# The low part of a weight half, made one step later on VectorE in a mixture-of-experts decoder layer

## The chip, the cores and the metric

The kernel runs on 1 core of one Trainium2 chip. The metric is the device time in microseconds of the whole program, the median over runs. All of it is one launch: a decoder layer with attention, a recurrent block and a mixture of experts.

## The reference, cut to what matters

```python
def _moe(h, w_router, e_bias, w_gate, w_up, w_down, ws_gate, ws_up, ws_down):
    ...
    scores = jax.nn.sigmoid(hf.astype(f32) @ w_router.astype(f32))
    ...
    _, idx = lax.top_k(jnp.where(emask, sel, -jnp.inf), TOP_K)
    ...
    def body(acc, blk):
        toks, bw, e = blk
        xb = hp[toks]
        yb = (jax.nn.silu(xb @ w_gate[e]) * (xb @ w_up[e])) @ w_down[e]
        return acc.at[toks].add(yb.astype(f32) * bw[:, None]), None
```

There are 2048 tokens of 1024 numbers, 64 experts of width 256, and each token goes to 8 experts. The pairs of token and expert are sorted by expert and padded to blocks of 128. With the inputs drawn here the routing gives 31 experts two blocks and 33 experts three, 161 blocks in all, and no expert has one.

## The kernel before, in words

The change lies in the expert stage, the function `experts`, which takes the span from about 886 to 2377 us. Its loop goes over the blocks in turns of two: block n = 0 of a turn (k = 0) is called an even step here, n = 1 an odd step. There are 162 steps. A step gathers 128 rows of h, forms G = x [gate | up] (128 x 512), H = silu(gate part) * up part * pair weight (128 x 256), transposes H and forms Y = H w_down (128 x 1024), which GpSimd adds to the sums in DRAM by a scatter.

Every product is made with numbers split in two, a high part rounded to fp32r and a low part, the difference. So a product takes three passes on TensorE: high by high, high by low, low by high. ScalarE makes the high parts, VectorE the low parts by a subtraction. This holds for the rows x (`xT_hi`, `xT_lo`), for the transposed H (`HT_hi` by line 2489, `HT_lo` by line 2590) and for the weights of an expert, in three pieces: piece 0 is the gate half of `gu_split`, piece 1 its up half, piece 2 the down weights (`d_hi`, `d_lo`). The subtraction of a weight piece is line 2528, called by `split(entry, n)` for piece n.

The weights sit in two raw slots and two split slots. At the first block of an expert the pieces of the *next* expert are split into the other slot. `when_first(engine, words[i], body)` is a branch at run time: it runs `body` only if block i is the first of its expert. In step s, `words[n]` is the block of the step, `words[n + 1]` the one behind it. For an expert whose first block is f, VectorE makes pieces 0 and 1 of the next expert at the end of step f - 2, and piece 2 early in step f.

All engines run through lists written by hand and meet on semaphores. TensorE's step is: the low pass of G for the next block (`gate_up_low`, line 2659), Y of this block (line 2697, whose third pass in each half reads `HT_lo`), the high passes of G for the block two steps on (`gate_up_high`, line 2645, which waits for the low parts of gate and up), and the H transposes of the next block (`turn_H`, line 2666, psH), in odd steps also transposes of the gathered rows (psX, psW). VectorE's step is:

```python
s.wait(dve, HThi_s)
nc.vector.tensor_tensor(HT_lo[:], ...)
when_first(dve, words[n], lambda: split(words[n], 2))
low_x(s.turn + 2, k)
...
product(s.n + 2, 1 - k, s.turn + 1 + k)
if k == 0:
    turn_x(s.turn + 2)
when_first(dve, words[n + 2], lambda: split(words[n + 2], 0))
when_first(dve, words[n + 2], lambda: split(words[n + 2], 1))
```

`product` makes H of the next block (line 2567), `turn_x` transposes the gathered rows of the odd blocks on VectorE (lines 2512 and 2514, only in even steps), after four gathers by GpSimd (line 1669) have landed. ScalarE's step is HT_hi, xT_hi, an index, silu, the high parts of gate and up where due (line 2444), the two halves of y, the high part of down where due. SP's queue reloads a raw slot's gate and up (line 2359) when the low parts of both are made (`gulo_s`), and its down weights when theirs is made.

Of the kernel before, what the change touches and what calls it, by code (L numbers as in the profile page):

```python
# [61 lines left out]
def carry_wait(eng, passed):  # L62


    eng.sem_inc(passed, 1)
# [2133 lines left out]
def experts(nc, passed, w_gate, w_up, w_down, ident, htab, hcut, sums, table, n_turns, idx, pidx, tails_s, xg, gi, gi_s, x_in, acc_out, gu, guhi_s, gulo_s, wgu, wd, loaded, y, si, added,  # L2199
# [6 lines left out]
    with ExitStack() as ctx:  # L2206
# [58 lines left out]
        def within(v, low, high):  # L2265
            return nc.s_assert_within(v, low, high, skip_runtime_bounds_check_because="the table's fields have these ranges")
# [29 lines left out]
        def entries(eng, first, n):  # L2296

            ap = table[0:1, first:first + n] if isinstance(first, int) else table[0:1, bass.ds(first, n)]
            return [Entry(v) for v in load(eng, ap, (1 << FIRST_BIT + 1) - 1)]
# [3 lines left out]
        def parts(raw, slot):  # L2303

            def piece(t, at, columns):
                return t[:, bass.ds(at, 1) if not isinstance(at, int) else slice(at, at + 1), :, columns].rearrange("p a k n -> p (a k) n")

            for h, columns in enumerate((slice(0, FE), slice(FE, 2 * FE))):
                yield piece(runs_view(wgu)[:, :, h], raw, slice(0, FE)), piece(gu_hi, slot, columns), piece(gu_lo, slot, columns)
            yield tuple(piece(t, at, slice(0, D)) for t, at in ((wd, raw), (d_hi, slot), (d_lo, slot)))  # L2310

        def when_first(eng, entry, body):

            with eng.If(entry.first() > 0):
                body()
            with eng.Else():
                eng.sem_inc(passed, 1)
# [186 lines left out]
        def _(dve):  # L2504
# [25 lines left out]
            block0, block1 = entries(dve, 0, 2)  # L2530
# [7 lines left out]
            def split(entry, n):  # L2538

                raw = within(entry.next() & 1, 0, 1)  # L2540
                src, hi, lo = list(parts(raw, 1 - entry.slot()))[n]
                if n == 2:
                    dve.wait_ge(dhi_s, entry.rank() + 1)
                else:
                    dve.wait_ge(guhi_s, entry.rank() * GU_SPLITS + n + 1)
                carry_wait(dve, passed)
                low(n, src, hi, lo)
# [32 lines left out]
            low_x(1, 1)  # L2580
            when_first(dve, block0, lambda: split(block0, 1))
            when_first(dve, block1, lambda: split(block1, 0))
            when_first(dve, block1, lambda: split(block1, 1))

            def body(i):
                words = entries(dve, i * TURN, TURN + 2)
                for n, s, k in steps(i):

                    s.wait(dve, HThi_s)
                    nc.vector.tensor_tensor(HT_lo[:], psH[:, 0:FE].rearrange("p (a b) -> p a b", a=2), HT_hi[:],  # L2590
                                            ALU.subtract).then_inc(HTlo_s, 1)
                    when_first(dve, words[n], lambda: split(words[n], 2))
                    low_x(s.turn + 2, k)
                    s.wait(dve, H_s)
                    if k == 0:
                        pair_weight(words[n + 2], s.turn + 2, 0)
                        pair_weight(words[n + 1], s.turn + 1, 1)
                    product(s.n + 2, 1 - k, s.turn + 1 + k)
                    if k == 0:
                        turn_x(s.turn + 2)  # L2600
                    when_first(dve, words[n + 2], lambda: split(words[n + 2], 0))
                    when_first(dve, words[n + 2], lambda: split(words[n + 2], 1))

            turns(dve, body)

        @block.tensor
# [733 lines left out]
```

## Time and profile before

| | |
|---|---|
| median of 3 runs | 2500.54 us (2498.16 to 2504.78) |
| the profiled execution | 2502.44 us, span 2500.6 us |
| TensorE (PE) busy | 2345.8 us, 94% of the span |
| VectorE (DVE) busy | 1659.6 us, 66% |
| ScalarE (ACT) busy | 1263.4 us, 51% |
| GpSimd (POOL) busy | 980.9 us, 39% |
| granted TensorE clock | 0.976 of full speed |
| DMA | 551.13 MB, mean 220 GB/s |

Busy time is the time in which an engine has an instruction under way; register and branch instructions don't count. The idle time of an engine that is not the bottleneck costs nothing by itself. Matmuls are pipelined, so the lengths of two neighbours overlap, and steps are best measured from start to start.

### The profile page before, as it was taken

What the parts mean: (1) busy time and instruction counts of PE and PEld (TensorE: products, weight loads), DVE (VectorE), ACT (ScalarE), POOL (GpSimd) and SP (SyncE); (2) the same over time, 40 slices, a digit from 0 to 9 for tenths busy, and PEclk for the clock granted to TensorE, in tenths of its full rate; (3) what the DMA queues carried; (4) which work ended last, traced back from release to release, by engine and by line L of the source; (5) the groups of instructions that cost most, each with busy time, mean ns of one, the idle gap of its engine ahead of it and who ended that gap; (6) DMA issues with size and microseconds to landing.
All of it is one profiled execution on the core that took longest, in us unless ns stands there. A gap on an engine that the chain in (4) does not pass through costs nothing. (4 is left out here: it accounts for less than half of the span.)

```text
span 2500.6 us, 49354 instructions
## 1 busy us (share of the span) xinstructions
PE 2345.8 (94%) x11266; PEld 1900.4 (76%) x11268; DVE 1659.6 (66%) x2220; ACT 1263.4 (51%) x2025; POOL 980.9 (39%) x772
## 2 busy tenths in 40 slices
PE   8899999989998799999999999999999999999966
PEld 6576777668886677888778887787878888887844
DVE  6685867758877766666666666656666657656337
ACT  4525253532325655555555555555655556655334
POOL 0010101011110155555555555555645556655437
PEclk9999999989998899999999999999999999999989
DMA  7243434465656479888897878888888789987796
GB/s 253 76 168 122 136 118 144 135 223 187 226 204 210 157 240 279 242 231 255 273 269 230 262 222 259 263 266 262 268 254 236 222 252 290 272 271 213 177 248 202
DMA packets 165327, 551.13 MB, mean 220 GB/s; under 512 B 31344, under 2 KB 56080, under 8 KB 144784
## 3 DMA queue, kind: packets, MB, share of 16 engines
q1 hardware_dynamic: 109696, 355.03, 39.9%
q0 software_dynamic: 54960, 195.27, 32.6%
q8 instruction: 36, 0.59, 0.1%
q14 instruction: 27, 0.22, 0.0%
q10 hardware_dynamic: 608, 0.02, 0.0%
HBM read 394.99 MB, written 155.25 MB: 220 GB/s over the span
## 5 line engine op out<-in xcount | busy, mean ns | idle before, releaser
L2645 PE MATMUL psG<-gu_split,xT_hi 128*128 x2624 | 626.2, 391 | 3.4 <-ACT xT_hi L2421 1.9
L2645 PEld LDWEIGHTS psG<-gu_split,xT_hi 128*128 128x128 f32 x2624 | 495.0, 189 | 107.6 <-issue 4.1
L1669 POOL DMA_INDIRECT xg<-hcut,gi x332 | 418.4, 1260 | 201.5 <-ACT gi L2432 113.9
L2659 PE MATMUL psG<-gu_split,xT_lo 128*128 x1304 | 342.3, 404 | 0.9 <-issue 0.9
L2590 DVE TENSOR_TENSOR HT_lo<-psH,HT_hi 128x256 fp32r<-128x256 f32 x162 | 68.7, 424 | 379.6 <-ACT HT_hi L2489 371.3
L2528 DVE TENSOR_TENSOR gu_split<-raw_gu,gu_split (+1 forms) x127 | 284.3, 2281 | 44.7 <-issue 27.0
L2659 PEld LDWEIGHTS psG<-gu_split,xT_lo 128*128 128x128 f32 x1304 | 232.9, 188 | 44.6 <-issue 2.5
L2406 POOL DMA_INDIRECT acc<-y,si x81 | 184.4, 2277 | 160.2 <-ACT y L2498 146.3
L2444 ACT ACTIVATE gu_split<-raw_gu x126 | 234.5, 1909 | 25.0 <-issue 18.3
L2697 PE MATMUL psY<-d_hi,HT_lo 128*128 x648 | 202.9, 394 | 31.7 <-DVE HT_lo L2590 31.5
L2489 ACT ACTIVATE HT_hi<-psH 128x256 fp32r<-128x256 f32 x162 | 62.2, 384 | 286.6 <-PE psH L2666 261.4
L2697 PE MATMUL psY<-d_hi,HT_hi 128*128 x648 | 201.8, 393 | 0.7 <-issue 0.5
L2697 PE MATMUL psY<-d_lo,HT_hi 128*128 x648 | 200.1, 390 | 0.0
L2512 DVE STREAM_TRANSPOSE xF<-xg 128x1024 f32<-128x1024 f32 x82 | 176.8, 2157 | 34.6 <-DMA xg<-hcut,gi 34.6
L1662 POOL DMA_INDIRECT xg<-htab,gi x83 | 81.8, 985 | 289.2 <-DVE pairw L2558 233.4
L2528 DVE TENSOR_TENSOR d_lo<-raw_d,d_hi (+1 forms) x64 | 146.7, 2293 | 44.4 <-issue 43.5
L2697 PEld LDWEIGHTS psY<-d_hi,HT_lo 128*128 128x128 f32 x648 | 120.0, 189 | 66.0 <-issue 42.5
L2406 POOL DMA_INDIRECT second<-y,si x81 | 145.8, 1800 | 26.3 <-issue 26.3
L2697 PEld LDWEIGHTS psY<-d_hi,HT_hi 128*128 128x128 f32 x648 | 121.0, 188 | 30.0 <-issue 3.9
L950 PE MATMUL psP<-xT_hi,wring 128*128 128x512 f32 x512 | 131.6, 407 | 11.2 <-ACT xT_hi L468 3.6
L2697 PEld LDWEIGHTS psY<-d_lo,HT_hi 128*128 128x128 f32 x648 | 121.9, 188 | 26.6
L418 POOL TENSOR_TENSOR OS<-QK 128x256 f32<-128x256 f32 x15 | 11.0, 735 | 316.4 <-ACT QK L560 316.4
(404 smaller groups left out, 4102.5 us busy)
## 6 DMA issues: line engine op xcount, KB each, us to landing
raw_gu<-in_w_gate_dram SPq DMA_DIRECT2D x64, 1024.0 KB
raw_gu<-in_w_up_dram SPq DMA_DIRECT2D x64, 1024.0 KB
raw_d<-in_w_down_dram SPq DMA_DIRECT2D x64, 1024.0 KB
wring<-split_d SPq DMA_DIRECT2D x24, 1024.0 KB, 5.7
second<-blank SPq DMA_DIRECT2D x17, 512.0 KB, 6.7
split_d<-wring POOLq DMA_DIRECT2D x8, 1024.0 KB, 4.2
raw_d<-mixed SPq DMA_DIRECT2D x16, 512.0 KB, 5.6
xt<-in_x_dram SPq DMA_DIRECT2D x16, 512.0 KB, 5.7
```

Source lines behind the costliest of these rows:

```text
L950: m = nc.tensor.matmul(u.tile[:], w_[:, w, k, :], xT[x_][:, k, :], start=(n == 0), stop=(n == len(passes) - 1))
L1662: nc.gpsimd.indirect_dma_start(out=to[:], out_offset=None, in_=htab, in_offset=bass.IndirectOffsetOnAxis(ap=at[:, 0:1], axis=0)).then_inc( ...
L1669: nc.gpsimd.indirect_dma_start(out=to[:, g, 0:PIECE], out_offset=None, in_=hcut.rearrange("r a w -> (r a) w"), in_offset=bass.IndirectOffs ...
L2406: nc.gpsimd.indirect_dma_start(out=sums[k], out_offset=bass.IndirectOffsetOnAxis(ap=si[k][:, 0:1], axis=0), in_=y[k][:], in_offset=None, c ...
L2444: nc.scalar.activation(dst, src, ACT.Copy).then_inc(done, 1)
L2489: nc.scalar.activation(HT_hi[:], psH[:, 0:FE].rearrange("p (a b) -> p a b", a=2), ACT.Copy).then_inc(HThi_s, 1)
L2512: nc.vector.transpose(xF[:, 0:KC, :].rearrange("p c (g j) -> p c g j", g=QUADS), xg[1][:, :, 0:FEATS].rearrange("p g (i c) -> p c g i", c=KC))
L2528: nc.vector.tensor_tensor(dst, src, hi, ALU.subtract).then_inc(dlo_s if n == 2 else gulo_s, 1)
L2590: nc.vector.tensor_tensor(HT_lo[:], psH[:, 0:FE].rearrange("p (a b) -> p a b", a=2), HT_hi[:], ALU.subtract).then_inc(HTlo_s, 1)
L2645: nc.tensor.matmul(psG[slot][:], xT_hi[slot][:, c, :], right[:, bass.ds(w, 1), c, :].rearrange("p a n -> p (a n)"), start=(n == 0 and c == ...
L2659: m = nc.tensor.matmul(psG[slot][:], xT_lo[slot][:, c, :], gu_hi[:, bass.ds(w, 1), c, :].rearrange("p a n -> p (a n)"), start=False, stop= ...
L2697: m = nc.tensor.matmul(psY[:, h, :], left[:, c, :], right[:, bass.ds(w, 1), c, h * 512:(h + 1) * 512].rearrange("p a n -> p (a n)"), start ...
```

## The change

The subtraction for piece 1, the up half, no longer follows that for piece 0 at the end of a step. It stands in the next step, directly behind HT_lo, under the same condition (there the same block is `words[n + 1]`). The one for the second block's expert in the prologue goes away, since the first step of the loop now makes it.

```diff
             when_first(dve, block0, lambda: split(block0, 1))
             when_first(dve, block1, lambda: split(block1, 0))
-            when_first(dve, block1, lambda: split(block1, 1))
...
                     nc.vector.tensor_tensor(HT_lo[:], psH[:, 0:FE].rearrange("p (a b) -> p a b", a=2), HT_hi[:],
                                             ALU.subtract).then_inc(HTlo_s, 1)
+                    when_first(dve, words[n + 1], lambda: split(words[n + 1], 1))
                     when_first(dve, words[n], lambda: split(words[n], 2))
                     low_x(s.turn + 2, k)
...
                     when_first(dve, words[n + 2], lambda: split(words[n + 2], 0))
-                    when_first(dve, words[n + 2], lambda: split(words[n + 2], 1))
```

On VectorE, at the start of the loop's body (the even step), the change puts the branch and the subtraction of piece 1 behind HT_lo; `-` is before, `+` the change, and lines shift by one:

```order
 L1126 REGISTER_ALU
-L2590 TENSOR_TENSOR HT_lo<-psH,HT_hi 128x256
+L2589 TENSOR_TENSOR HT_lo<-psH,HT_hi 128x256
+L2314 REGISTER_ALU
+L2314 COMPARE_AND_BRANCH
+L2545 REGISTER_ALU x2
+L2545 ISA
+L2528 REGISTER_ALU x3
+L2528 ISA
+L2528 REGISTER_ALU
+L2528 ISA x2
+L2528 TENSOR_TENSOR gu_split<-raw_gu,gu_split 128x8x256
```

HT_lo itself stays first in the even step; ahead of the branch for the down weights there now stands one more.

On VectorE, where the even step ends and the odd step begins, behind the subtraction of piece 0:

```order
 L2314 UNCONDITIONAL_BRANCH
 L2316 UNCONDITIONAL_BRANCH
+L2589 TENSOR_TENSOR HT_lo<-psH,HT_hi 128x256
 L2314 COMPARE_AND_BRANCH
 L2545 REGISTER_ALU x2
```

The two rows at the end belong to the branch of piece 1, which is followed by its subtraction. A few rows on, behind that subtraction, HT_lo stood before:

```order
 L2314 UNCONDITIONAL_BRANCH
 L2316 UNCONDITIONAL_BRANCH
-L2590 TENSOR_TENSOR HT_lo<-psH,HT_hi 128x256
-L2314 REGISTER_ALU
 L2314 COMPARE_AND_BRANCH
 L2543 REGISTER_ALU x3
```

So in the odd step HT_lo moved ahead of the subtraction of piece 1, and nothing else changed places. No other engine's order changes.

## Rows read from the trace of the kernel before

**Rows 1.** waits, whole span (engine, tile and line, awaited: us in total, times, longest)

```profile
PE psY L2697 <- DVE HT_lo L2590: 31.5, 21, 2.3
```

**Rows 2.** timeline, one late step (start us, length us, engine, line, operation; idle before)

```profile
1569.65 0.38 PE L2666 MATMUL psH<-ident,H 128*128 128x128 f32 x2
...
1570.62 0.38 ACT L2489 ACTIVATE HT_hi<-psH 128x256 fp32r<-128x256 f32 x1 [1.69 <-PE psH L2666]
...
1572.15 2.29 DVE L2528 TENSOR_TENSOR d_lo<-raw_d,d_hi  x1 [0.69 <-issue]
...
1573.85 3.73 ACT L2444 ACTIVATE gu_split<-raw_gu  x2 [0.53 <-issue]
...
1576.27 2.18 DVE L2512 STREAM_TRANSPOSE xF<-xg 128x1024 f32<-128x1024 f32 x1
...
1578.56 4.45 DVE L2528 TENSOR_TENSOR gu_split<-raw_gu,gu_split  x2
1579.09 0.38 PE L2666 MATMUL psH<-ident,H 128*128 128x128 f32 x2
...
1579.51 0.38 ACT L2489 ACTIVATE HT_hi<-psH 128x256 fp32r<-128x256 f32 x1 [0.89 <-PE psH L2666]
...
1582.93 0.42 DVE L2590 TENSOR_TENSOR HT_lo<-psH,HT_hi 128x256 fp32r<-128x256 f32 x1
1583.26 1.22 DVE L2520 TENSOR_TENSOR xT_lo<-xF,xT_hi 128x1024 fp32r<-128x1024 f32 x1
1583.49 0.70 PE L2697 MATMUL psY<-d_hi,HT_lo 128*128 x2 [1.27 <-DVE HT_lo L2590]
...
1584.39 0.48 DVE L2567 SCALAR_TENSOR_TENSOR H<-psG,pairw,sg 128x256 f32<-128x256 f32 x1
...
1589.03 0.38 PE L2666 MATMUL psH<-ident,H 128*128 128x128 f32 x2
```

**Rows 3.** timeline, an odd step that waits for nothing

```profile
1521.39 0.39 PE L2666 MATMUL psH<-ident,H 128*128 128x128 f32 x2
...
1529.83 0.38 PE L2666 MATMUL psH<-ident,H 128*128 128x128 f32 x2
```

**Rows 4.** timeline, an odd step in which the low part is slightly late

```profile
931.03 0.39 PE L2666 MATMUL psH<-ident,H 128*128 128x128 f32 x2
...
933.59 0.47 DVE L2590 TENSOR_TENSOR HT_lo<-psH,HT_hi 128x256 fp32r<-128x256 f32 x1
...
939.77 0.38 PE L2666 MATMUL psH<-ident,H 128*128 128x128 f32 x2
```

**Rows 5.** timeline and windows, the longest wait and TensorE's clock behind it

```profile
2281.16 1.19 PE L2697 MATMUL psY<-d_hi,HT_lo 128*128 x2 [2.29 <-DVE HT_lo L2590]
...
2281.20:2284.70 3.50, 3.50 (x9) 2.79 (x10) 1.34 (x2) 0.69 (x2) 2.59 (x4) 0.52 0.89 197
```

**Rows 6.** timeline, two even steps, each behind an odd step without a wait

```profile
1105.89 0.38 PE L2666 MATMUL psH<-ident,H 128*128 128x128 f32 x2
...
1107.92 0.38 ACT L2489 ACTIVATE HT_hi<-psH 128x256 fp32r<-128x256 f32 x1 [2.76 <-remote]
...
1922.96 0.38 PE L2666 MATMUL psH<-ident,H 128*128 128x128 f32 x2
...
1925.68 0.38 ACT L2489 ACTIVATE HT_hi<-psH 128x256 fp32r<-128x256 f32 x1 [3.44 <-remote]
...
1933.48 0.39 PE L2666 MATMUL psH<-ident,H 128*128 128x128 f32 x2
```

**Rows 7.** windows, six experts in a row without a wait

```profile
2052.00:2159.00 107.00, 107.00 (x511) 88.96 (x510) 79.01 (x84) 70.66 (x108) 69.85 (x42) 1.00 0.96 296
```

**Rows 8.** timeline, GpSimd's scatter beside VectorE and alone

```profile
1097.99 3.15 POOL L2406 DMA_INDIRECT acc<-y,si  x1 [4.08 <-ACT y L2498]
...
1099.88 1.26 DVE L2520 TENSOR_TENSOR xT_lo<-xF,xT_hi 128x1024 fp32r<-128x1024 f32 x1
...
2110.81 1.59 POOL L2406 DMA_INDIRECT acc<-y,si  x1 [1.51 <-ACT y L2498]
```

## The prediction

> **What bounds the kernel now.** The profile's page comes first: TensorE is busy for 94% of the span, so only time in which it waits can be won. The waits of TensorE on other engines come second. In the expert stage one of them counts: the product with the low part of H (line 2697) waits for VectorE's subtraction (line 2590) 21 times, 31.5 us in all, 2.3 us at most [rows 1]. The timeline around one such wait comes third [rows 2]. A step runs from one pair of H transposes on TensorE to the next. The even step starts at 1569.65 and lasts 9.44 us. Near its end VectorE turns the next rows (1576.27) and makes two low parts in one go, 4.45 us from 1578.56. The odd step begins at 1579.09; ScalarE has the high part of H started at 1579.51, so VectorE could go on at about 1579.9, but it starts HT_lo only at 1582.93, directly behind the second low part. TensorE has the products before it done and sits idle for 1.27 us until 1583.49. The step lasts 9.94 us; an odd step without a wait lasts 8.44 [rows 3]. So a listed wait of 1.27 costs 1.50, which is 0.23 more than the list says.
>
> Why 21 times: the inputs give 31 experts of two blocks and 33 of three. VectorE is late when an even step holds three low parts, the one of the down weights (1572.15 in [rows 2]) and the two that follow, which needs an expert of two blocks that starts at an even block. Leaving out the first expert, there are 21. Where the even step has only the last two, HT_lo starts 2.56 us after the transposes at the latest, and the step takes 8.74, or 0.30 too long [rows 4]; six steps look like this. Of this I also read the limit: HT_lo may start about 2.56 - 0.30 = 2.26 us after the transposes before TensorE feels it. The longest wait has a price of its own: behind it the granted clock was 0.52 for 3.5 us [rows 5], its lower level of 1.2 GHz, which loses about 1.7 us.
>
> **The change, part by part.** The same instructions are issued in the same number; one subtraction of 2.29 us per expert moves from ahead of HT_lo to behind it.
>
> *What goes.* The two low parts take 4.45 us and one alone takes 2.29 [rows 2], so HT_lo comes 2.16 us earlier: at 1580.77, or 1.68 after the transposes, where 2.26 is allowed. All waits up to 2.16 vanish: 31.5 + 21 x 0.23 = 36.3 us. The six slightly late steps give 6 x 0.30 = 1.8, the slow clock 1.7. Together 39.8 us. About three waits lie near or above 2.16; I leave 0.3 us in each, 1.0 in all.
>
> *What the moved part delays.* In the odd step it now stands ahead of the low part of x and of H, but there it stood already, since all three are behind it in VectorE's order today as well. HT_lo alone overtakes. Their starts in [rows 2] stay, while TensorE arrives 1.5 us sooner. H is made by 1584.39 + 0.48 = 1584.9, and TensorE's transposes would come at 1589.03 - 1.50 = 1587.5: 2.6 us of cover. In steps where VectorE was idle ahead of HT_lo, the part begins 0.69 us behind it (the gap that such a branch leaves, 1572.15 in [rows 2]) and pushes x and H by some 3 us. The even step of [rows 2] already holds a low part at that very place and its H is in time, so this costs nothing.
>
> *One more untaken branch.* Each step now tests one condition more between HT_lo and the down weights' low part. No row has the price of an untaken branch alone. It lies between 0 and the 0.69 of a gap that holds a taken one; I take 0.3, since much less is executed. In the even step this pushes the chain (down part, x, H, turn, first low part) and puts HT_lo at 1.98 of 2.26. At 0.69 it would be 2.37, and 21 steps lose 0.1 each.
>
> *TensorE's own wait.* gate_up_high asks for both low parts, but for the block two steps on. With two blocks or more in every expert the moved part is ready one whole step ahead. Nothing is lost there.
>
> *SP's queue.* The gate and up reload waits for the second low part, so it starts later: by HT_lo alone in [rows 2], some 0.4 us, and by up to 4 where VectorE was idle ahead of HT_lo. The slot is read again two experts on: ScalarE's split at 1573.85 recurs after 19.4 us per expert, so 29 us pass, and 26 without the waits. The three megabytes at the 296 GB/s of [rows 7] need about 11 us. That covers the delay, and costs nothing. Nor does the faster pace run into the DMA: six experts of two blocks from odd starts ran back to back at 0.96 DMA share with TensorE busy for 107.00 of 107.00 us [rows 7].
>
> *What is late next.* ScalarE. In the even step behind a late odd step its high part of H starts 0.97 us after the transposes [rows 2]. Behind an odd step without a wait it starts 2.03 after them, and once 2.72 [rows 6], with nothing in the timeline to explain it. That delay runs down VectorE's chain to the next HT_lo. With 0.97 the next HT_lo is at 1.98, no wait. With 2.03 it is at 3.04, or 0.8 too late. The change turns all late odd steps into clean ones, so it brings this about itself. Per step the cost is between 0 and 0.8; a late step helps the next one, so I take the middle, 0.4, for 21 steps: 8.4 us. At 2.72 TensorE itself waits: that even step took 10.52 instead of 9.44, which is 1.08 [rows 6]. I expect two more of these, 2.2 us; the bounds are none and five.
>
> *Sum.* 39.8 - 1.0 - 8.4 - 2.2 = 28.2 us. The profiled execution took 2502.44 (span 2500.6), so it would take 2474.2. The median of the three runs is 1.9 lower, 2500.54, and goes to about **2472 us**.
>
> **Rivals.** (a) *The whole wait goes:* ScalarE stays at 0.97. 38.8 us are won, 2462. For it: the late starts may hang on where the row gathers stand against the loop's top, and that moves too. Against it: every clean odd step with this pattern that I read has ScalarE late.
>
> (b) *Half comes back:* ScalarE's delay at its upper bound, 21 x 0.8 + 5 x 1.08 = 22.2 us, so 16.6 are left, 2484; with the branch at 0.69 as well, 2486.
>
> (c) *The gathers come late.* GpSimd's scatter took 3.15 us and ended at 1101.14, in the moment in which VectorE's low part of x ended (1099.88 + 1.26); alone it takes 1.59 [rows 8]. So VectorE's subtractions hold GpSimd back, and behind the scatter stand the four gathers whose rows VectorE turns in the even step. Today these subtractions end 5.4 us into a step of 9.94 (at 1584.5, by 1583.26 in [rows 2] and its 1.2 us), 4.5 before the next transposes; afterwards 5.8 into 8.44, which is 2.6 before. If all of the 1.9 us reached the turn at 1576.27 and then HT_lo, less the 0.28 of room, 21 steps would lose 34 us: 2506, about no change. It decides once the gathers land later than 6.6 us into the even step. Against it: the window of [rows 7] has this contention and no wait. The Trainium skill, SBUF — State Buffer, Who interferes with whom, says that a VectorE instruction with two SBUF inputs contends only with a GpSimd instruction that reads SBUF, and infers that descriptor generation is not held up by tensor_tensor. By that inference this rival costs nothing and the sum stays 2472; the row of 3.15 us speaks against it.
>
> (d) *The other side, slower:* ScalarE's high part of H starts at 2.7 in every even step behind an odd one that now holds such a low part. There are 37. TensorE loses 37 x 1.08 = 40 us, HT_lo 21 x 0.8 = 17, against 38.8 won: 18 slower, 2519. It decides somewhere between 2.03 and 2.72 us behind the transposes. Against it: 2.03 is what [rows 6] shows for an ordinary one, and only a few are at 2.7.
>
> (e) *No real move:* HT_lo stays late because the first low part alone ends too late. The rows say 1.68 against 2.26, so this would need a chain a microsecond longer than shown: 2500.
>
> **How the numbers follow.** Forecast 0.60, (a) 0.20, (b) 0.09, (c) 0.04, (d) 0.04, (e) 0.03. A measurement of this kernel can tell about 0.3%, 7.5 us, from no change. Faster by more: the first three, 0.89. Within: (c) and (e), 0.07. Slower: (d), 0.04. The range runs from the full gain with a little over, 2460, to (b) with the branch, 2487; it leaves out (c), (d), (e) and edges.
>
> **What would show it.** In the changed profile the wait of line 2697 for HT_lo should fall from 31.5 to under 12 us. HT_lo in odd steps should begin about 1.7 to 3.0 us after the transposes, followed directly by one low part of 2.29; only one should stand ahead of it. Odd steps of the late kind should last 8.4 to 9.2 instead of 9.94. ScalarE's high part in even steps should start 1 to 2 us after the transposes, and its waits and TensorE's on it should have grown. The turn should rarely wait for gathers in even steps behind late ones. I am wrong if odd steps stay above 9.5, if the turn waits for DMA where it did not, or if many even steps last over 10 us.

## The result, and the profile after

| | before | changed |
|---|---|---|
| median, beside each other | 2500.1 us (2498.16 to 2504.78, 4 runs) | 2458.78 us (2457.51 to 2465.86, 4 runs) |
| ratio, 95% interval | | 0.9838, 0.9815 to 0.9861 |
| the profiled execution's span | 2500.6 us | 2455.7 us |
| expert stage, from the first to the last H transposes | 886.0 to 2377.6: 1491.6 us | 877.4 to 2332.6: 1455.3 us |
| TensorE busy | 2345.8 us | 2333.2 us |
| granted clock | 0.976 | 0.977 |

The change won 41.3 us where 28 were forecast, and the median lies just below the range. The two profiled executions differ by 44.9 us: 36.3 in the expert stage and 8.6 ahead of it. The 8.6 are not the change's. In the other profiled executions below, whatever the kernel, the stage began anywhere from 875.5 to 885.8 us (the changed kernel's own at 876.0 to 883.8), and the part behind it was equal (123.0 and 123.1).

Waits of TensorE in the changed kernel, the row that answers to [rows 1] (31.5 us, 21 times):

```profile
PE psY L2696 <- DVE HT_lo L2589: 3.6, 5, 1.0
```

The timeline of the same even and odd step as [rows 2], in the changed kernel:

```profile
1542.83 0.38 PE L2665 MATMUL psH<-ident,H 128*128 128x128 f32 x2
...
1543.24 0.38 ACT L2489 ACTIVATE HT_hi<-psH 128x256 fp32r<-128x256 f32 x1 [1.15 <-PE psH L2665]
1543.66 0.42 DVE L2589 TENSOR_TENSOR HT_lo<-psH,HT_hi 128x256 fp32r<-128x256 f32 x1 [2.82 <-issue]
1545.14 2.29 DVE L2528 TENSOR_TENSOR d_lo<-raw_d,d_hi  x1 [1.06 <-issue]
...
1551.56 2.29 DVE L2528 TENSOR_TENSOR gu_split<-raw_gu,gu_split  x1
1552.34 0.38 PE L2665 MATMUL psH<-ident,H 128*128 128x128 f32 x2
...
1553.73 0.44 DVE L2589 TENSOR_TENSOR HT_lo<-psH,HT_hi 128x256 fp32r<-128x256 f32 x1
1554.33 2.29 DVE L2528 TENSOR_TENSOR gu_split<-raw_gu,gu_split  x1 [0.15 <-issue]
...
1557.67 0.48 DVE L2567 SCALAR_TENSOR_TENSOR H<-psG,pairw,sg 128x256 f32<-128x256 f32 x1
...
1560.76 0.38 PE L2665 MATMUL psH<-ident,H 128*128 128x128 f32 x2
```

One low part stands ahead of HT_lo in the odd step, one behind it. HT_lo starts 1.39 us after the transposes (1553.73 - 1552.34), where [rows 2] has 3.84, and the step lasts 8.42 instead of 9.94. H is ready 2.6 us ahead of the next transposes.

What was not expected stands in the even steps. The same two as in [rows 6], where ScalarE's high part of H came 2.03 and 2.72 us after the transposes, look like this in the changed kernel:

```profile
1092.71 0.38 PE L2665 MATMUL psH<-ident,H 128*128 128x128 f32 x2
...
1093.13 0.38 ACT L2489 ACTIVATE HT_hi<-psH 128x256 fp32r<-128x256 f32 x1 [1.15 <-PE psH L2665]
...
1884.43 0.38 PE L2665 MATMUL psH<-ident,H 128*128 128x128 f32 x2
...
1884.92 0.39 ACT L2489 ACTIVATE HT_hi<-psH 128x256 fp32r<-128x256 f32 x1 [1.21 <-PE psH L2665]
...
1893.89 0.39 PE L2665 MATMUL psH<-ident,H 128*128 128x128 f32 x2
```

It comes at 0.42 and 0.49, and the second step takes 9.46 instead of 10.52. In the changed kernel the high part starts at 0.51 or earlier in 79 of 80 even steps; in the kernel before it was later than 0.7 in 37 of them.

The releaser at the end of the row names the cause. In [rows 6] it is "remote", an event without an instruction that just ended; here it is the transposes themselves. The trace's semaphore events say it outright (the times are from the start of the transposes, in the even step of 1105.89 in the kernel before and of 1092.71 in the changed one):

```
event                                   before   changed
TensorE: H transposes done              2.01     0.40
TensorE: pair weights transposed        2.73     0.51
TensorE: x transposes done, first half  2.82     1.24
TensorE: x transposes done, second half 2.90     2.73
TensorE: low pass of G done             3.24     3.24
```

ScalarE started at 2.03 in the first, right behind the signal. So it was never late itself. TensorE's completion signal for the transposes was, while its matmul records and the signal of the next product were on time in both. This is called the late signal below. (In the changed kernel the signals behind the first two can be held as well, 2.73 where 1.40 is the rule; that touches the high part of x alone.)

The chain of VectorE hangs on it. In the even step of [rows 2] the signal is 0.55 us late. HT_lo and the down part stand 0.55 later for it, and so should x, H, the turn, the low parts and the HT_lo that TensorE waits for in the odd step; how much of it arrives there is measured by the unused subtraction below.

### The profile page after: what moved, and what is told of

It is laid out like the page before. It is cut to its first block and busy times, and to the rows that moved or that the text cites. A ratio compares the mean times of both kernels' runs of the same rounds, so it can differ in the third digit from the quotient of the medians.

```text
span 2455.7 us, 49353 instructions
## 1 busy us (share of the span) xinstructions
PE 2333.2 (95%) x11267; PEld 1898.1 (77%) x11268; DVE 1670.5 (68%) x2220; ACT 1268.9 (52%) x2025; POOL 980.6 (40%) x772
## 5 line engine op out<-in xcount | busy, mean ns | idle before, releaser
L1669 POOL DMA_INDIRECT xg<-hcut,gi x332 | 447.1, 1347 | 212.5 <-ACT gi L2432 122.0
L2528 DVE TENSOR_TENSOR gu_split<-raw_gu,gu_split (+1 forms) x127 | 289.8, 2282 | 78.1 <-issue 67.9
L2406 POOL DMA_INDIRECT acc<-y,si x81 | 146.9, 1813 | 136.8 <-ACT y L2498 115.9
L2512 DVE STREAM_TRANSPOSE xF<-xg 128x1024 f32<-128x1024 f32 x82 | 177.7, 2166 | 21.0 <-DMA xg<-hcut,gi 20.6
L2528 DVE TENSOR_TENSOR d_lo<-raw_d,d_hi (+1 forms) x64 | 146.7, 2293 | 63.7 <-issue 62.9
L2406 POOL DMA_INDIRECT second<-y,si x81 | 156.1, 1927 | 25.8 <-issue 24.2
```

Source lines behind the costliest of these rows:

```text
L1669: nc.gpsimd.indirect_dma_start(out=to[:, g, 0:PIECE], out_offset=None, in_=hcut.rearrange("r a w -> (r a) w"), in_offset=bass.IndirectOffs ...
L2406: nc.gpsimd.indirect_dma_start(out=sums[k], out_offset=bass.IndirectOffsetOnAxis(ap=si[k][:, 0:1], axis=0), in_=y[k][:], in_offset=None, c ...
L2512: nc.vector.transpose(xF[:, 0:KC, :].rearrange("p c (g j) -> p c g j", g=QUADS), xg[1][:, :, 0:FEATS].rearrange("p g (i c) -> p c g i", c=KC))
L2528: nc.vector.tensor_tensor(dst, src, hi, ALU.subtract).then_inc(dlo_s if n == 2 else gulo_s, 1)
```

## The experiments

Times are medians; the kernel before was timed beside each set of runs.

### Which half of the deferral does it, and is it the reload

Four kernels of one set, the kernel before at 2499.54 (2493.86 to 2509.29). The first is the changed kernel again.

> The change as it is, on this chip beside the others. 2457 to 2466 us. If the stages ahead of the expert stage run level with before here, then 8.6 us of the 44.9 us between the two first profiles are chance of these two executions; if they are again some 9 us shorter, the change acts there too.

2462.86, ratio 0.985 (0.982 to 0.987). The stage took 1457.5.

The second defers piece 1 only into odd steps:

```diff
+                    if k == 1:
+                        when_first(dve, words[n + 1], lambda: split(words[n + 1], 1))
...
-                    when_first(dve, words[n + 2], lambda: split(words[n + 2], 1))
+                    if k == 1:
+                        when_first(dve, words[n + 2], lambda: split(words[n + 2], 1))
```

> Only the up low part that used to stand at the end of an even step is moved behind HT_lo of the odd step; the one at the end of an odd step stays where it was. Theory A (the gain is HT_lo overtaking a low part in the 21 crowded odd steps): nearly all of the gain of the change, 30 to 45 us against before. Theory B (a good part of the gain comes from the even step, where the moved low part lets something else go earlier): less than 25 us.

2460.35, ratio 0.984 (0.982 to 0.987): the whole gain. It doesn't tell the overtaking of HT_lo from the late signal, since the signal is on time here too in all but five even steps.

The third defers it only into even steps (the same with `k == 0`).

> The mirror: only the up low part at the end of an odd step is moved into the next even step. Theory A: no change, within 4 us of before, and 21 waits for HT_lo of 1.2 to 2.3 us stay. Theory B: 10 us or more are won.

2513.03, ratio 1.005 (1.003 to 1.007): 13 us slower, where at most 4 were expected. The late odd step of [rows 2] in it:

```profile
1582.82 0.38 PE L2668 MATMUL psH<-ident,H 128*128 128x128 f32 x2
...
1586.98 0.40 DVE L2589 TENSOR_TENSOR HT_lo<-psH,HT_hi 128x256 fp32r<-128x256 f32 x1
...
1587.53 0.70 PE L2699 MATMUL psY<-d_hi,HT_lo 128*128 x2 [1.58 <-DVE HT_lo L2589]
...
1593.10 0.38 PE L2668 MATMUL psH<-ident,H 128*128 128x128 f32 x2
```

HT_lo starts at 4.16 where [rows 2] has 3.84, and the step takes 10.28 instead of 9.94. The only thing added to VectorE's crowded even steps is one untaken branch. Ahead of the down part the idle time is 1.06 us in the even step of the changed kernel above, against 0.69 in [rows 2]: an untaken branch costs 0.37 us there. Here it lies on the path of every late step. Three stretches ran at a granted clock of 0.50 behind their waits (3.4, 6.8 and 3.4 us), against one in the kernel before, and the longest step took 14.31. That isn't all of the loss: of the 16.4 us that the stage grew, 9.1 lie in odd steps and 7.3 in even ones, of which seven lasted 9.9 to 11.5 us, against four of 10.0 to 10.6 in the kernel before.

The fourth is the kernel before with a later reload. SP waits in addition until ScalarE has taken up the next expert's down split:

```diff
+                            sp.wait_ge(free_s, before)
...
+                act.sem_inc(free_s, 1)
```

> VectorE's order is that of before. SP's reload of gate and up waits also for ScalarE to reach the down split of the next expert, so it starts about 2.8 us ahead of the even step's transposes instead of 5.6. Theory R (ScalarE's late high part of H at the loop's top comes from the reload's traffic, and the change cured it by issuing the reload later): the high part of H starts 0.4 to 0.6 us after the transposes in all even steps; the four even steps of 10.0 to 10.6 us are gone and the crowded odd steps shorten by about 0.5 us each, 10 to 16 us won in all. Rival (the lateness follows VectorE's or GpSimd's order): ScalarE stays at 1.0 to 2.9 us, time within 4 us of before.

2515.6, ratio 1.007 (1.005 to 1.010). The gate reload now started 2.9 us ahead of the even transposes in most steps and the up reload 1.4, instead of 5.6 and 5.1, and HT_hi was still at about 0.95 behind waits. Behind short odd steps it was mostly at 2.9 to 3.0, where the kernel before has 1.4 to 2.9. So a later reload doesn't cure the signal, but it isn't without effect on it: it came later still. The time was expected within 4 us of the kernel before and is 16 us longer.

### Traffic, place, and an earlier reload

Four kernels of a second set, the kernel before at 2500.57 (2493.23 to 2507.74). First the kernel before with an eighth of the gate and up bytes. It leaves out the other seven eighths and multiplies with weights left over from earlier experts, so it serves for timing alone:

```diff
+                        if sm is not down_in:
+                            dst, src = dst[:, 0:1], src[:, 0:1]
```

> The kernel before, but each reload of gate and up weights moves an eighth of its bytes (the experts from the third on are computed with weights left over from earlier ones in the other seven eighths). In the kernel before, TensorE's signal that the H transposes are done comes late in even steps that begin an expert: ScalarE's HT_hi starts 0.97 us after the transposes behind a wait and 1.4 to 2.9 behind a clean odd step, where 0.42 is the rule. Theory T (traffic: the signal is held while the reload's packets run): HT_hi starts at 0.42 to 0.5 in all even steps, even steps last 9.44, the four of 10.0 to 10.6 are gone. The 21 waits for HT_lo stay at 1.3 to 1.5, since they come from VectorE's order, so the time falls only by the 4 us of those even steps and by some half-clock stretches: 2490 to 2498. Theory B (the state of the engines, not the traffic): HT_hi starts as late as before, 2497 to 2503.

2502.47, ratio 1.002 (1.000 to 1.003). The even step of 1105.89 in it:

```profile
1097.03 0.38 PE L2669 MATMUL psH<-ident,H 128*128 128x128 f32 x2
...
1099.50 0.39 ACT L2492 ACTIVATE HT_hi<-psH 128x256 fp32r<-128x256 f32 x1 [3.21 <-remote]
```

HT_hi starts 2.47 us after the transposes, 2.03 in the kernel before. The bytes of the gate and up reload are not the cause.

Then piece 1 in odd steps only, behind the product of H instead of behind HT_lo (the line of e1 moved below `product(...)`):

> As the version that defers piece 1 only into odd steps, but with the piece behind the product of H instead of directly behind HT_lo. H is then ready about 4 us before TensorE's transposes, as in the kernel before, and not 2.6. Theory T: the early H does not matter; HT_hi stays at 0.42 in even steps or moves with the reload, which now starts some 2 us later; 2455 to 2463, as the version deferring into odd steps (2460.35). Theory B (a signal held because TensorE's sequencer is further back when H is early): HT_hi is at 0.97 to 2.9 again in the even steps behind the 37 odd steps, several even steps take 10.5, 2468 to 2485. In both, the low part of x and H come earlier in odd steps, so GpSimd's scatter and gathers run beside one subtraction less and the seven odd steps that were late through the gathers should be fewer than seven, worth 2 to 4 us.

2462.52, ratio 0.986 (0.983 to 0.988). HT_hi stayed at 0.42 in all even steps that begin an expert, so an early H does not bring the late signal back. The second part of the expectation failed: the 37 odd steps lost 10.5 us in all, not less than the changed kernel's 5.1. The reload starts only 1.5 to 1.9 us ahead of the even transposes in it.

Then the changed kernel with its gate reload released by piece 0 alone, piece 1 signalling on a semaphore of its own (`gulo1_s`):

```diff
-                            sp.wait_ge(gulo_s, 2 * before)
+                            sp.wait_ge(gulo_s if sm is gate_in else gulo1_s, before)
```

> The changed kernel, but SP reloads the gate weights as soon as piece 0 alone is made (a semaphore of its own for piece 1). The gate reload then starts about 6 us before the even transposes, where the changed kernel has it 3.7 before and the kernel before 5.6. If the late signal in even steps comes from a reload that is under way since more than 5 us, HT_hi goes back to 1 to 2.9 in even steps and the time rises to 2468 to 2485. If VectorE's order alone decides, HT_hi stays at 0.42 and the time within 4 us of the changed kernel's 2459 to 2463. TensorE and SP test one semaphore more, which should cost nothing.

2455.32, ratio 0.982 (0.980 to 0.985). The signal stayed on time and the stage took 1447.5, which is 81 x (9.44 + 8.43), the pace of TensorE alone. It shows what the changed kernel still lost. An even and an odd step with late gathers in the changed kernel:

```profile
963.34 0.33 SPq L2359 DMA_DIRECT2D raw_gu<-in_w_gate_dram  x1
963.91 0.33 SPq L2359 DMA_DIRECT2D raw_gu<-in_w_up_dram  x1
...
966.55 0.38 PE L2665 MATMUL psH<-ident,H 128*128 128x128 f32 x2
...
975.02 2.14 DVE L2512 STREAM_TRANSPOSE xF<-xg 128x1024 f32<-128x1024 f32 x1 [1.94 <-DMA xg<-hcut,gi]
975.99 0.38 PE L2665 MATMUL psH<-ident,H 128*128 128x128 f32 x2
...
979.45 0.41 DVE L2589 TENSOR_TENSOR HT_lo<-psH,HT_hi 128x256 fp32r<-128x256 f32 x1
...
980.01 0.70 PE L2696 MATMUL psY<-d_hi,HT_lo 128*128 x2 [0.88 <-DVE HT_lo L2589]
...
985.58 0.38 PE L2665 MATMUL psH<-ident,H 128*128 128x128 f32 x2
```

The same steps with the early gate reload (rows from its second measurement):

```profile
960.24 0.33 SPq L2360 DMA_DIRECT2D raw_gu<-in_w_gate_dram  x1
...
962.83 0.33 SPq L2360 DMA_DIRECT2D raw_gu<-in_w_up_dram  x1
...
966.77 0.38 PE L2670 MATMUL psH<-ident,H 128*128 128x128 f32 x2
...
973.20 2.18 DVE L2515 STREAM_TRANSPOSE xF<-xg 128x1024 f32<-128x1024 f32 x1
...
976.21 0.38 PE L2670 MATMUL psH<-ident,H 128*128 128x128 f32 x2
...
984.62 0.38 PE L2670 MATMUL psH<-ident,H 128*128 128x128 f32 x2
```

Above, both reloads are issued 3.2 and 2.6 us ahead of the transposes, in the same moments as the gathers of the odd block, and the turn waits 1.94 us for those; HT_lo comes 3.46 us into the odd step, which takes 9.59. Below, the gate reload is issued 6.5 us ahead, the turn starts at 6.43 without a wait, and the odd step takes 8.41. In the changed kernel seven odd steps are of the first kind (8.5 to 9.7 us). That it is the reload, and not gathers that GpSimd issues late, shows in the even step at 1182.65: its four gathers are issued at the same offsets as with the early gate reload (within 0.05 us), and the turn starts at 8.54 instead of 6.46.

The seven steps are not all that the early reload won. Of the 7.8 us between 1455.3 and 1447.5, 2.9 lie in even steps, the most in this one:

```profile
2081.24 0.38 PE L2665 MATMUL psH<-ident,H 128*128 128x128 f32 x2
...
2083.05 2.11 PE L2658 MATMUL psG<-gu_split,xT_lo 128*128 x8 [0.43 <-issue]
...
2091.43 0.38 PE L2665 MATMUL psH<-ident,H 128*128 128x128 f32 x2
```

The low pass of G starts 1.81 us after the transposes, where 1.13 is the rule, and no engine is named that it waits for. The trace's records of TensorE's sequencer have its read of the turn's block words (`entries`) there from 0.20 to 1.21 us, and in the next even step from -0.61 to -0.28. Such late starts sum to 2.9, 2.9 and 2.5 us in three profiles of the changed kernel beside the late signal and to 0.8 and 0.6 with the early gate reload. Why the reload's time bears on them is open.

Last of the set, both pieces in the odd step behind the product:

```diff
                     product(s.n + 2, 1 - k, s.turn + 1 + k)
+                    if k == 1:
+                        when_first(dve, words[n + 1], lambda: split(words[n + 1], 0))
+                        when_first(dve, words[n + 1], lambda: split(words[n + 1], 1))
...
-                    when_first(dve, words[n + 2], lambda: split(words[n + 2], 0))
-                    when_first(dve, words[n + 2], lambda: split(words[n + 2], 1))
+                    if k == 1:
+                        when_first(dve, words[n + 2], lambda: split(words[n + 2], 0))
+                        when_first(dve, words[n + 2], lambda: split(words[n + 2], 1))
```

> Both pieces 0 and 1, for an expert that starts at an even block, are made in the odd step ahead of it behind the product of H; the even step that begins an expert holds the down piece alone. VectorE's odd step is then HT_lo, low part of x, H, 4.45 us of low parts: it ends about 8.3 of 8.43 us after the transposes, the even step ends with the turn at about 8.6 of 9.44. No HT_lo is late if both fit: the 37 odd steps at 8.43 and the even ones at 9.44 give 81 x 17.87 = 1447.5 us for the stage, 8 below the changed kernel's 1455.3: 2450 to 2456. If the even step's HT_lo comes late (allowed about 2.3 us after the transposes) by 0.5 us in 37 steps, it gives 2465 to 2475. If Theory B holds, HT_hi is late again in these even steps, 2465 to 2485.

2453.92, ratio 0.982 (0.979 to 0.984), the stage at 1446.6. The odd step of [rows 2] (rows from its second measurement):

```profile
1550.21 0.38 PE L2670 MATMUL psH<-ident,H 128*128 128x128 f32 x2
...
1551.27 0.40 DVE L2590 TENSOR_TENSOR HT_lo<-psH,HT_hi 128x256 fp32r<-128x256 f32 x1
...
1554.10 4.49 DVE L2528 TENSOR_TENSOR gu_split<-raw_gu,gu_split  x2
1558.62 0.38 PE L2670 MATMUL psH<-ident,H 128*128 128x128 f32 x2
```

HT_lo starts at 1.06, and both low parts fit in between the product and the next transposes. VectorE's turn waits for gathers far more often here than in the changed kernel (54 times, 129.2 us, against 19 and 20.6), but no low part of a weight stands between the turn and HT_lo, and no odd step is late.

### The late signal alone

In the kernels so far a late signal nearly always goes with an odd step ahead in which VectorE makes no low part of a weight, or only ones that have ended 6 us ahead of the transposes, and a signal on time with one made later than that. The exceptions are counted further below. A third set, the kernel before at 2499.12 (2493.94 to 2503.89), tests this with work that does nothing. The kernel before gets one unused subtraction of the size of a piece, and its own pieces stay where they are:

```diff
+                    if k == 1:
+                        when_first(dve, words[n + 1], lambda: nc.vector.tensor_tensor(idle[:], idle[:], idle[:], ALU.subtract))
```

> The kernel before, with a subtraction of the size of one weight piece (128 x 2048, on a buffer that nobody uses) behind HT_lo in the odd step ahead of an expert that starts at an even block; the order of the real pieces is that of before. In all kernels with a late signal of the H transposes no low part of a weight stood in these odd steps, in all without it one did. Theory V (VectorE's work at that place sets where GpSimd and the transfers stand at the loop's top, and with it the signal): HT_hi starts at 0.42 in the even steps behind, as in the changed kernel, and the four even steps of over 10 us are gone, 4 us won, while the added work in the waiting odd steps (low part of x and H 2.5 us later, H at about 8.3 of 9.94) costs 0 to 10: 2496 to 2510. Theory O (the order and signals of the real pieces): HT_hi stays at 0.95 behind waits and 1.4 to 2.9 behind clean odd steps. In both the 21 waits for HT_lo stay.

2480.06, ratio 0.992 (0.990 to 0.994): the kernel before becomes 19 us faster by added work. Its waits, its odd step of [rows 2] and its even step of 1105.89:

```profile
PE psY L2701 <- DVE HT_lo L2592: 18.2, 22, 1.4
...
1102.21 0.38 PE L2670 MATMUL psH<-ident,H 128*128 128x128 f32 x2
...
1102.63 0.38 ACT L2490 ACTIVATE HT_hi<-psH 128x256 fp32r<-128x256 f32 x1 [1.15 <-PE psH L2670]
...
1568.64 0.38 PE L2670 MATMUL psH<-ident,H 128*128 128x128 f32 x2
...
1572.11 0.42 DVE L2592 TENSOR_TENSOR HT_lo<-psH,HT_hi 128x256 fp32r<-128x256 f32 x1
1572.44 2.29 DVE L2595 TENSOR_TENSOR idle<-idle 128x2048 f32<-128x2048 f32 x1
...
1572.68 0.70 PE L2701 MATMUL psY<-d_hi,HT_lo 128*128 x2 [0.90 <-DVE HT_lo L2592]
...
1578.23 0.38 PE L2670 MATMUL psH<-ident,H 128*128 128x128 f32 x2
```

Theory V holds for the signal: HT_hi is at 0.42 in all even steps behind such an odd step. It was not that this execution met no late signals: in the last two even steps of the loop, with no subtraction ahead, HT_hi was at 1.41 and 1.53. The time fell by more than expected, because the waits of TensorE shrank as well, from 31.5 to 18.2 us, on average from 1.50 to 0.83, about what the signal had cost VectorE's chain. The stage went from 1491.6 to 1473.1. So the late signal cost the kernel before at least 18.5 us, since the unused subtraction may have a price of its own. The order of the changed kernel takes another 17.8, down to 1455.3, and the early gate reload 7.8, to 1447.5.

In the same set stood the changed kernel, 2461.15 (ratio 0.985, 0.983 to 0.987), the early gate reload, 2452.54 (0.982, 0.980 to 0.984), and both pieces behind the product, 2451.67 (0.981, 0.980 to 0.983). The last two beat the changed kernel by 9 us on one chip. None of their runs in this set (2449.11 to 2456.66) reaches the changed kernel's lowest, 2457.52.

> The changed kernel once more, beside the two that come next, on one chip. 2457 to 2464, as its first two measurements (2458.78 and 2462.86).

> The version in which SP reloads the gate weights as soon as piece 0 is made, again, beside the changed kernel. Theory L (the changed kernel's remaining loss in the expert stage, some 8 us over the floor of 81 x 17.87 = 1447.5, comes from the later reload, whose packets delay the gathers): 4 to 9 us faster than the changed kernel of this call, and VectorE's turn in even steps never starts later than 6.7 us after the transposes. If its first measurement (2455.32) was chance: within 3 us of the changed kernel.

> The version in which both pieces 0 and 1 are made in the odd step behind the product, again, beside the changed kernel. Its stage ran at the floor (1446.6), so 4 to 10 us faster than the changed kernel of this call and within 3 us of the version with the early gate reload.

### How the idle work does it: not settled

Two kernels were to tell GpSimd from VectorE and long from short work: the kernel before with a memset between GpSimd's gathers, and with a quarter-sized unused subtraction behind the product.

```diff
+                            if q == 2:
+                                pool.wait_ge(idle_s, s.turn + 1)
+                                carry_wait(pool, passed)
+                                nc.gpsimd.memset(idle[:], 0.0).then_inc(idle_s, 1)
```

> The kernel before, with a memset of 128 x 1024 on GpSimd (a buffer that nobody uses) between the second and the third of the four gathers of each odd step; VectorE's list is that of before. It tests the way through GpSimd: in the kernels with the signal on time one of GpSimd's transfers in the odd step is stretched to 1.6 to 3.3 us beside VectorE's subtraction, in those with a late signal the four gathers go out 1.25 us apart, 0.95 long, up to the loop's top. Theory P (that unbroken row of gathers holds the signal): HT_hi starts at 0.42 in the even steps that were late, and the time falls to 2478 to 2492, less what the later gathers cost VectorE's turn. Theory Q (the subtraction on VectorE itself is what matters, with GpSimd no part of it): HT_hi stays at 0.95 behind waits and 1.4 to 2.9 behind clean odd steps; 2500 to 2515, since the gathers come about 1 us later and the turn waits for them.

> The kernel before, with a small unused subtraction on VectorE (128 x 512, about 0.7 us, a quarter of the one that cured the late signal) behind the product of H in the same odd steps. If any work of VectorE late in the odd step is enough, HT_hi starts at 0.42 in the even steps behind and the time falls as with the large one, or some more, since the low part of x and H are not held up: 2474 to 2482. If its length or what it does to GpSimd's transfers matters, the signal stays late in most of these steps: 2495 to 2502.

2475.93 and 2474.84, but the kernel before itself took 2476.05 (2472.91 to 2480.09, 19 runs) in this fourth set, on a chip on which it had taken 2499.12 in the third. Both ratios are 1.000 (0.999 to 1.001), and in both profiles no signal was late, not even in the last two even steps. The kernel before was not profiled in this set; that its signal was on time too is read from its time. The condition had gone. A fifth set, on another chip, added the changed kernel, and met the same, the kernel before at 2474.92 (2472.15 to 2479.47, 20 runs):

> In the last set of runs the kernel before took 2476 us instead of 2500, on a chip on which it had taken 2499 in the set ahead, and no signal of the H transposes was late in the two kernels profiled there (HT_hi at 0.42 in every even step). So the late signal is a condition that a set of runs has or has not. Where the kernel before is at 2494 to 2504 beside this run, the changed kernel takes 2457 to 2464, 38 to 42 less. Where the kernel before is at about 2476, Theory S (half of the gain is the signal, half the overtaking of HT_lo) expects the changed kernel at 2450 to 2460, only 17 to 25 less.

2458.37 (2450.50 to 2464.61), ratio 0.993 (0.991 to 0.996): 16.6 us won, as Theory S said, just below its 17 to 25.

> The kernel before with a memset on GpSimd between the second and third gather of each odd step, again, since its first set of runs had no late signal to remove. With the kernel before at 2494 to 2504: Theory P (the unbroken row of gathers holds the signal) expects HT_hi at 0.42 in nearly all even steps and 2474 to 2490; Theory Q (only VectorE's subtraction matters) HT_hi at 0.95 to 2.9 as before and 2497 to 2510. With the kernel before at 2476: no difference again.

> The kernel before with a small unused subtraction (128 x 512) behind the product in the odd step, again. With the kernel before at 2494 to 2504: if any late work of VectorE is enough, HT_hi at 0.42 and 2474 to 2484; if the length matters, late in most steps and 2495 to 2502. With the kernel before at 2476: no difference again.

2474.72 and 2475.69, ratios 1.000. The even step of 1105.89 and the waits in the second of them, where the idle subtraction has nothing to cure:

```profile
PE psY L2701 <- DVE HT_lo L2592: 18.1, 21, 1.3
...
1101.36 0.38 PE L2670 MATMUL psH<-ident,H 128*128 128x128 f32 x2
...
1101.78 0.38 ACT L2490 ACTIVATE HT_hi<-psH 128x256 fp32r<-128x256 f32 x1 [1.15 <-PE psH L2670]
```

The signal is on time and TensorE's wait is 18.1 us, the 18.2 of the cured kernel. So two ways lead to the same kernel before at about 2476 to 2480: take the late signal away by work on VectorE, or meet a set of runs without it.

A last run drew the condition once more, with both pieces behind the product:

> The version in which both pieces 0 and 1 are made in the odd step behind the product, a third time, in a set of its own. Its expert stage ran at the floor of 81 x 17.87 = 1447.5 us and had no late signal, so its time should not depend on the condition of the set: 2449 to 2455, whether the kernel before takes 2500 or 2475 beside it. If it also gains where the signal is on time, it goes to 2440 to 2447.

2451.92, ratio 0.981 (0.979 to 0.984), with the kernel before at 2498.65: the condition was back.

Over the 15 profiles of the sets with it (the two of the comparison itself among them) the count is this. In 1026 even steps a weight-sized subtraction of VectorE had ended within the last 4.5 us ahead of the transposes: 7 had HT_hi later than 0.7 us. In the other 174 it was late in 155. In the five profiles of the two sets without it, 0 of 400 were late.

The 174 also hang on how long the odd step ahead lasted. Behind 91 shorter than 9.2 us the signal was late in 88 (HT_hi up to 3.0), behind 66 of 9.2 to 10.9 us in all (HT_hi mostly at 0.8 to 1.0), and behind 17 of 11.0 us or more in one alone. So VectorE's work need not be what shields the signal in itself; whatever holds it may need time to pass. What the condition is, and by what way the subtraction acts, stays open: a pause in GpSimd's gathers and the small subtraction would have told more, and met the condition in neither of their sets.

## Why the prediction was right and where it was wrong

**What goes: right in size.** The forecast was 39.8 us for all waits, six slightly late steps and the slow clock. The 37 odd steps in question lay 40.6 over 8.43 each in the kernel before and 5.1 over in the changed one. The 5.1 are seven late steps of another cause, and with the early gate reload nothing is left. (The trace has seven slightly late steps, with HT_lo at 2.63 at the latest, where six and 2.56 were read.) But the number is not all the overtaking's, as the forecast had it: in the kernel before with the unused subtraction, where HT_lo still stands behind both low parts, the odd steps lay only about 24 us over. The rest of the 40.6 went with the late signal alone. HT_lo overtook just one low part, 2.29 us stands ahead of it, and H has the 2.6 us of cover worked out. The residue of 1.0 near the longest waits did not occur: in the odd step of [rows 2] HT_lo starts at 1.39 where 1.98 was assumed.

**What is late next, ScalarE: wrong, and in sign.** This is the step that failed. It charged 8.4 us for a high part of H that comes late in even steps and 2.2 for more even steps of 10.52, 10.6 in all, because every clean odd step of this pattern showed it. The runs showed that ScalarE is not late. TensorE's completion signal was, almost only in even steps whose odd step ahead held no late weight subtraction, and the moved piece puts exactly that there. The change did not bring the lateness about but removed it: HT_hi at 0.42 instead of 0.97 and more. The 10.6 did not come, and the 3.8 us that even steps over 9.44 cost the kernel before went as well (four of them took 10.0 to 10.6; the prediction had seen one). Rival (a) had this outcome with HT_hi staying at 0.97, and its 2462 was the nearest. The word "remote" in [rows 6] was the hint. I read the row as a late engine instead of asking what had released it.

**SP's queue, "costs nothing": wrong by about 8 us.** The term looked only at whether the weights would be there in time, and they were. It did not ask what the later transfer runs into. It falls on the gathers of the odd block, whose rows VectorE turns at 6.4 us, which cost 5.1 us, and TensorE's low pass of G started late at the loop's top for another 2.9. Releasing the gate reload earlier took the stage from 1455.3 to 1447.5, and both measurements of it were faster. The mechanism is that of rival (c), the turn late through the gathers, with another cause: in the version with the early reload, GpSimd's scatter stands beside the same subtractions and no step is late.

**The untaken branch: right.** 0.3 us taken; idle time ahead of the down part went from 43.5 to 62.9 us over 63 of them, 0.31 each, 0.37 in even steps. Its weight showed only where it stood in a path with no room, in the version that defers into even steps alone. That one lost 13 us, of which the branch is a part that no run separates.

**Sum of the parts.** 28.2 forecast, plus 10.6 that did not come, plus 3.8 of before's even steps, plus 1.0 of residue, plus 0.8 by which the late odd steps were larger than read, less 5.1 for the gathers and 2.9 for TensorE's late starts: 36.4, against 36.3 in the stage. The rest of the 41.3 in the medians is within how executions differ ahead of the stage.

**The forecast's size depends on a condition that it did not know.** With the late signal the changed kernel took 41.3, 36.7 and 38.0 us less than the kernel before beside it, and without it 16.6. The changed kernel itself took 2458 to 2463 in all. So about 17 us are what the new order wins by itself, and the rest of the 41 is the late signal, which no row quoted in the prediction let it price. That the time lies so near rival (a) is luck in part: (a) had ScalarE stay at 0.97, and nothing of a signal that comes back on time.

**GpSimd beside VectorE.** The scatter of the odd steps took 2.3 us on average in the kernel before (up to 4.89) and 1.8 in the changed one (up to 3.59), the long ones all beside subtractions of VectorE, against 1.59 alone [rows 8]. The inference of the Trainium skill, SBUF — State Buffer, Who interferes with whom, that such a subtraction does not hold up descriptor generation, does not agree with these rows, unless the longer scatters come from its read of the index tile in SBUF, which no run here separates. Nor does a run separate what the longer scatters cost.

## What to carry to other kernels

When a row says that an engine starts late, look at what released it, and at the semaphore's own event, before charging the engine: a completion signal can be what is late, and then its cost runs down every chain that hangs on it. When a step that frees a buffer is moved later, ask what the reload will run beside, not only whether it arrives in time; a separate semaphore for the first half of the buffer won 9 us here. Late data costs only what stands behind it on the path: with both low parts moved away from behind the turn, waits of 129 us in all cost nothing. Time the kernel before in each set of runs, since half of a gain measured against it can be a condition that comes and goes.

## What the runs showed of the hardware

- TensorE's completion signals of the transposes at the loop's top arrived 0.4 to 2.6 us late in 155 of 174 even steps without a weight-sized subtraction in the last 4.5 us ahead, and in 7 of 1026 with one, while in the step looked at ScalarE's signal and TensorE's next one (low pass of G, 3.24 us) were on time. An unused 2.29 us subtraction on VectorE in the odd step ahead removed it. An eighth of the reload's bytes, or a reload 2.7 to 3.7 us later, did not.
- It was there in four sets of runs and the first comparison, and absent in the profiles of two sets, once on the chip that had just shown it: 2499 against 2476 us for the same kernel.
- An untaken branch at run time on VectorE cost 0.22 us (odd steps) to 0.37 us (even steps) between two instructions, 0.31 on average over 63.
- Two reloads of 1 MB issued about 3 us ahead of the loop's top made VectorE wait up to 2.0 us for the gathers issued beside them; with the first issued 6.5 us ahead no odd step was late.
